# The down product of an expert moved one round later, next to the next expert's transpositions

## The reference, cut to what matters

```python
aff = jax.nn.softmax((xt @ w_router).astype(jnp.float32), axis=-1)
gate, idx = lax.top_k(aff.T, cap)          # cap = 64 tokens per expert and sequence
xe = xt[idx]
g = jnp.einsum('ecd,edf->ecf', xe, w_gate)
u = jnp.einsum('ecd,edf->ecf', xe, w_up)
ye = jnp.einsum('ecf,efd->ecd', jax.nn.silu(g) * u, w_down) * gate[..., None]
y = jnp.zeros_like(xt).at[idx.reshape(-1)].add(ye.reshape(-1, shp[-1]))
```

## Time and profile before

| | |
|---|---|
| Time, median of 3 runs (lowest to highest) | 2575.97 us (2575.56 to 2576.26) |
| The profiled execution: its own time, and its span | 2580.33 us, 2578.4 us |
| Busy, share of the span | PE 97%, PEld 54%, DVE 56%, ACT 21%, POOL 28% |
| The experts' stages, about | 604 to 1249 us and 1926 us to the end |

### The profile page before, as it was taken

How to read it: one execution, slowest core, us unless ns; L and a number is a source line. 1 busy time by engine, 2 the same in 40 slices (tenths; PEclk the granted TensorE clock), 3 DMA queues, 4 the chain that set the end, 5 groups by cost and what they waited for, 6 DMA issues and landing times. The chain is left out here.

```text
span 2578.4 us, 37067 instructions
## 1 busy us (share of the span) xinstructions
PE 2501.9 (97%) x13964; PEld 1383.5 (54%) x13964; DVE 1447.2 (56%) x2210; ACT 553.5 (21%) x1400; POOL 732.4 (28%) x797
## 2 busy tenths in 40 slices
PE   8999999999999999999799999999989999999998
PEld 4456556445555555565344554454446565555554
DVE  2465456347866767765125332533258767668674
ACT  2164146111111111111102330332111111111112
POOL 2276358114122121120004530553022121121212
PEclk9999999999999999999899999999989999999999
DMA  6100030337999999997600112014248999999996
GB/s 200 27 7 16 1 147 10 122 134 294 335 356 340 344 355 332 353 349 261 242 28 17 54 58 93 17 46 160 98 172 315 352 350 332 355 345 346 353 336 247
DMA packets 177342, 534.91 MB, mean 207 GB/s; under 512 B 32464, under 2 KB 47312, under 8 KB 177232
## 3 DMA queue, kind: packets, MB, share of 16 engines
q1 hardware_dynamic: 166432, 499.34, 51.7%
q0 software_dynamic: 10800, 34.09, 5.8%
HBM read 490.39 MB, written 44.56 MB: 207 GB/s over the span
## 5 line engine op out<-in xcount | busy, mean ns | idle before, releaser
L1858 PE MATMUL bank<-ring,arena 128*64 128x256 f32 x4096 | 479.8, 382 | 2.4 <-DVE arena L2134 1.9
L1869 PE MATMUL bank<-ring,arena 128*128 128x512 f32 x1024 | 451.3, 599 | 1.8 <-issue 0.9
L917 PE MATMUL bank<-ring,arena 128*128 128x512 f32 (+1 forms) x1024 | 429.8, 576 | 1.7 <-DMA ring<-in_w_in_cd 0.9
L1858 PEld LDWEIGHTS bank<-ring,arena 128*64 128x64 f32 x4096 | 291.8, 137 | 168.3 <-issue 30.2
L1570 POOL TENSOR_SCALAR arena<-arena 128x512 f32<-128x512 f32 (+2 forms) x256 | 328.0, 1298 | 185.6 <-DVE arena L1446 177.4
L1858 PE MATMUL bank<-arena 128*64 128x256 f32 x3072 | 364.6, 379 | 0.0
L934 PE MATMUL bank<-arena,ring 128*128 128x512 f32 x752 | 330.1, 597 | 4.0 <-DVE arena L1402 4.0
L1869 PEld LDWEIGHTS bank<-ring,arena 128*128 128x128 f32 x1024 | 193.2, 191 | 245.6 <-issue 244.5
L917 PEld LDWEIGHTS bank<-ring,arena 128*128 128x128 f32 x1024 | 193.2, 192 | 208.1 <-issue 201.3
L2191 POOL DMA_INDIRECT residual<-arena x30 | 83.4, 2779 | 741.7 <-DVE arena L2101 741.7
L1858 PEld LDWEIGHTS bank<-arena 128*64 128x64 f32 x3072 | 222.4, 137 | 109.7 <-issue 0.6
(11 more groups left out here) (215 smaller groups left out, 2210.2 us busy)
## 6 DMA issues: line engine op xcount, KB each, us to landing
ring<-in_w_gate SPq DMA_DIRECT2D x64, 2048.0 KB, 9.4
ring<-in_w_up SPq DMA_DIRECT2D x64, 2048.0 KB, 10.4
ring<-in_w_down SPq DMA_DIRECT2D x64, 2048.0 KB, 7.9
ring<-in_w_in_cd SPq DMA_DIRECT2D x6, 2048.0 KB, 17.3
ring<-in_x_in SPq DMA_DIRECT2D x16, 512.0 KB, 4.3
residual<-ring SPq DMA_DIRECT2D x16, 512.0 KB, 2.8
normed<-ring SPq DMA_DIRECT2D x16, 512.0 KB, 2.6
ring<-residual SPq DMA_DIRECT2D x16, 512.0 KB, 6.1
```

The lines of the kernel that those rows point to most:

```text
L917: mm = eng.matmul(bank[banks_of(piece)[k]][0:rows, 0:wide], lhs(c), rhs(c), start=(c == 0), stop=(c == chunks - 1))
L1858: mm = eng.matmul(bank[b][64 * h:64 * h + 64, first_column:first_column + 256], tokens[:, c, :], weights[:, c, 256 * h:256 * h + 256], sta ...
L1869: mm = eng.matmul(bank[6 + b][:, :], lhs[:, 4 * half + c, :], piece[k][:, c, b * BANK:(b + 1) * BANK], start=(half == 0 and c == 0), stop= ...
```

## The change

The down product lags by two rounds instead of one: a round is now g(e) in one piece, down(e-2), h(e-1), u(e). There is one more round: round 16 holds down(14) and h(15), round 17 down(15). The down weights of expert 15 are loaded into buffers 0 and 1, which the last gate product has left. On VectorE and ScalarE the copy to hT stands behind y instead of ahead of the weight differences and of silu. SyncE loads down(e-1) where it loaded down(e), and in the first layer fetches the next mixer's pieces in the order 2, 4, 5, 0, 1, 3 instead of 0, 1, 2, 3, 4, 5, with `first_x` between 5 and 0. In the last layer the residual's tiles go to buffers 4 and 5. The core of the diff:

```diff
-            lags = {"h0": 1, "h1": 1, "down lo": 1, "down hi": 1, "hT": 1, "y": 1, "index": 1, "gate": 1,
+            lags = {"h0": 1, "h1": 1, "hT": 1, "down lo": 2, "down hi": 2, "y": 2, "index": 2, "gate": 2,
...
-            pe_names = ["g1", "g6", "g2", "g7", "g5", "h0", "h1", "g3", "g4", "down lo", "down hi",
+            pe_names = ["g1", "g6", "g2", "g7", "g5", "g3", "g4", "down lo", "down hi", "h0", "h1",
                         "u1", "u6", "u2", "u7", "u5", "u3", "u4"]
...
-                xt, yt = (ring[:, k * PIECE:(k + 2) * PIECE].rearrange("p (n d) -> p n d", n=TILES) for k in (0, 2))
+                xt, yt = (ring[:, k * PIECE:(k + 2) * PIECE].rearrange("p (n d) -> p n d", n=TILES) for k in (4, 2))
...
-                for k in range(4):
-                    load(0, k, 1)
-                with eng.Fori(1, E - 1) as e:
+                def load_last_down(k):
+
+                    eng.wait_ge(pe_s.sem, pe_s.after(freed[k], E - 1))
+                    eng.dma_start(piece[k], at(w_down, (E - 1 + layer * E) * (D * F) + k * (D * F // 2), [[F, P], [P * F, 4], [1, F]])
+                                  ).then_inc(piece_in[k], 16)
+
+                for e in range(2):
+                    for k in range(4):
+                        load(e, k, 1)
+                with eng.Fori(2, E - 1) as e:
                     for k in (0, 1):
                         load(e, k, 1)
                     for k in (4, 5):
-                        load(e, k, 0)
+                        load(e, k, -1)
                     for k in (2, 3):
                         load(e, k, 1)
-                for k in (4, 5):
-                    load(E - 1, k, 0)
+                load_last_down(0)
+                load(E - 1, 4, -1)
+                load_last_down(1)
+                load(E - 1, 5, -1)
                 if first:
-                    for k in range(2):
-                        eng.wait_ge(pe_s.sem, pe_s.after(freed[k], E - 1))
-                        follow(eng, k)
                     eng.wait_ge(pe_s.sem, pe_s.after("u4", E - 1))
                     eng.dma_start(first_gain, at(norm_mix, (layer + 1) * D, [[0, P], [1, D]])).then_inc(first_in, 16)
                     follow(eng, 2)
+                    for k in (4, 5):
+                        eng.wait_ge(pe_s.sem, pe_s.after(freed[k], E - 2))
+                        follow(eng, k)
                     eng.wait_ge(scattered, 16 * (E - 1))
                     eng.dma_start(first_x, at(residual, 0, [[D, P], [1, D]])).then_inc(first_in, 16)
-                    for k in range(3, RING):
-                        eng.wait_ge(pe_s.sem, pe_s.after(freed[k], E - 1))
+                    for k in range(2):
+                        eng.wait_ge(pe_s.sem, pe_s.after(("down lo", "down hi")[k], E - 1))
                         follow(eng, k)
+                    follow(eng, 3)
...
                     if "g1" not in left_out:
                         eng.wait_ge(dve_s.sem, dve_s.after("xT", e))
                         products("g", "s4", "tg2")
+                        last_products("g", "tg4")
+                    if "down lo" not in left_out:
+                        eng.wait_ge(act_s.sem, act_s.after("hT", e - 2))
+                        eng.wait_ge(dve_s.sem, dve_s.after("hT", e - 2))
+                        eng.wait_ge(act_s.sem, act_s.after("y", e - 3))
+                        eng.wait_ge(dve_s.sem, dve_s.after("y", e - 3))
+                        product(hT, 0 if is_end(e) else 4, 0, "down lo", e - 2)
+                        product(hT, 1 if is_end(e) else 5, 1, "down hi", e - 2)
```

More of the change, by code:

```diff
@@ L1783, in is_end, with behind, ahead @@
             def is_end(e):
-                return isinstance(e, int) and e == E
+                return isinstance(e, int) and e == E + 1
             def rounds(steps, eng, body):
-                late = [m for m in steps.names if lags.get(m) == 1]
                 early = [m for m in steps.names if lags.get(m) == -1]
-                tail = [m for m in steps.names if lags.get(m) != 1]
-                steps.part(late)
-                body(0, 0, late)
+                def behind(rounds):
+                    return [m for m in steps.names if lags.get(m, 0) >= rounds]
+                def ahead(rounds):
+                    return [m for m in steps.names if lags.get(m, 0) < rounds]
+                steps.part(behind(1))
+                body(0, 0, behind(1))
+                steps.part(behind(2))
+                body(1, 1, behind(2))
                 steps.part()
-                body(1, 1, ())
-                with eng.Fori(1, E // 2 - 1) as pair:
+                body(2, 0, ())
+                body(3, 1, ())
+                with eng.Fori(2, E // 2 - 1) as pair:
                     for j in range(2):
@@ L1800, in rounds @@
                 body(E - 1, 1, early)
-                steps.part(tail)
-                body(E, 0, tail)
+                steps.part(ahead(1))
+                body(E, 0, ahead(1))
+                steps.part(ahead(2))
+                body(E + 1, 1, ahead(2))
             def sp(eng):
@@ L1913, in body @@
                             pe_s.done(f"h{i}", mm)
[L1914 to L1920, removed]
                     if first and is_end(e):
                         eng.wait_ge(choice_made, 1)
-                        eng.wait_ge(act_s.sem, act_s.after("y", e - 1))
-                        eng.wait_ge(dve_s.sem, dve_s.after("y", e - 1))
+                        eng.wait_ge(act_s.sem, act_s.after("y", e - 2))
+                        eng.wait_ge(dve_s.sem, dve_s.after("y", e - 2))
                         for k in range(2):
-                            eng.matmul(bank[2 + k][:, :], choice, y[1 - j][0:64, k * 512:(k + 1) * 512], start=True, stop=True).then_inc(placed, 1)
+                            eng.matmul(bank[2 + k][:, :], choice, y[j][0:64, k * 512:(k + 1) * 512], start=True, stop=True).then_inc(placed, 1)
                     if "u1" not in left_out:
@@ L1977, in body @@
                     if "y" not in left_out:
[L1979 to L1981 removed]
+                        eng.wait_ge(pe_s.sem, pe_s.after("down hi", e - 2))
+                        eng.wait_ge(pool_s.sem, pool_s.after("gate", e - 2))
+                        act_s.done("y", eng.activation(y[j][:, 0:512], bank[6][:, :], ACT.Copy, scale=gate[j]))
+                    if "hT" not in left_out:
+                        eng.wait_ge(pe_s.sem, pe_s.after("h0", e - 1))
+                        act_s.done("hT", eng.activation(hT[:, :, 0:64], bank[0][:, :].rearrange("p (c t) -> p c t", t=64), ACT.Copy))
                     if "u p1" not in left_out:
@@ L2040, in body @@
                 def body(e, j, left_out):
-                    if "hT" not in left_out:
-                        eng.wait_ge(pe_s.sem, pe_s.after("h1", e - 1))
-                        dve_s.done("hT", eng.tensor_copy(hT[:, :, 64:128], bank[1][:, :].rearrange("p (c t) -> p c t", t=64)))
                     if last and is_end(e):
@@ L2097, in body @@
                         combine("g", 3, e + 1)
+                    if "tg2" not in left_out:
+                        for n in (2, 4):
+                            combine("g", n, e + 1)
                     if "y" not in left_out:
-                        eng.wait_ge(pe_s.sem, pe_s.after("down hi", e - 1))
-                        eng.wait_ge(pool_s.sem, pool_s.after("gate", e - 1))
-                        dve_s.done("y", eng.tensor_scalar(y[1 - j][:, 512:1024], bank[7][:, :], gate[1 - j], None, ALU.mult))
+                        eng.wait_ge(pe_s.sem, pe_s.after("down hi", e - 2))
+                        eng.wait_ge(pool_s.sem, pool_s.after("gate", e - 2))
+                        dve_s.done("y", eng.tensor_scalar(y[j][:, 512:1024], bank[7][:, :], gate[j], None, ALU.mult))
+                    if "hT" not in left_out:
+                        eng.wait_ge(pe_s.sem, pe_s.after("h1", e - 1))
+                        dve_s.done("hT", eng.tensor_copy(hT[:, :, 64:128], bank[1][:, :].rearrange("p (c t) -> p c t", t=64)))
                     if first and is_end(e):
```

58 lines of the change are left out of this document (26 added, 32 removed).

## The result

| | before | changed |
|---|---|---|
| Median of 8 runs each (lowest to highest) | 2577.45 us (2575.56 to 2581.12) | 2583.35 us (2581.58 to 2586.72) |
| Ratio, with its 95% interval | | 1.0024 [1.0015, 1.0034] |
| Profiled execution: its time, its span | 2580.33, 2578.4 us | 2584.28, 2582.5 us |

The change costs 5.9 us, 0.24%, with an interval of 3.9 to 8.8 us. I had forecast +1.9 us. The time lies inside my range, just outside what I called no change.

The account below looks back on a forecast made before the run. TensorE was taken to bound the rounds, other chains the ends. Rounds -9.0, round 1 +9.0, clock +2.0, layer 1's end -7.0, program's end +6.9 gave +1.9 us: median 2577.9 us, range 2571 to 2586.

Parts of the forecast that it names:

- what I called no change: Whole kernel: a median within 0.2%, 5.2 us, of the one before, that is 2570.8 to 2581.1 us; chance 0.59.
- rounds: Rounds 1 to 15 of each layer: one change of TensorE's form less saves 0.30 us a round, -9.0 us in all.
- The bound that let the price hang on the down product: Rounds: if the form change's price hangs on down, only h's 0.15 us a round is saved, -2.3 us per layer.
- round 1: Round 1 of each layer: without a down product TensorE waits 1.75 and 2.7 us in up, +9.0 us over both.
- clock: Behind round 1's two waits: TensorE's clock may fall, 1.0 us per layer, +2.0 in all, bounds 0 and 4.
- end of layer 1: Layer 1's end and next mixer: TensorE's 2.19 us wait goes, scatter and rows come earlier, -7.0 us, bounds -3.7 and -7.5.
- rival 3: Mixer behind layer 1: gains only the earlier start's 3.6 us if rows don't pass the weights, 2581.2 us; chance 0.10.
- the end of the program: Last layer's end: y(14) comes 12.1 us later, its scatter takes 5.0 instead of 10.16 us: +6.9 us, bounds +5.3 and +12.1.
- Rival 2: Program's end: the scatter stays at 10.16 us because reading and adding rows takes its time, 2583.1 us; chance 0.10.

Follow-up runs that it names:

- e3: The changed kernel with transpositions h back in the middle of the gate product, the down product left late: 2598.24 us, 1.0083.
- e4: The changed kernel with up block 6 waiting for tu2, two up copies ahead of silu, and hT last on ScalarE: 2575.67 us, 0.9996.
- e5: The changed kernel with the next mixer's weight piece 3 asked for right behind piece 2 in layer 1's end: 2579.38 us, 1.0009.
- e6: The changed kernel without expert 14's scatter in the last layer, tile loads waiting for u(15), tile buffers swapped: 2569.63 us, 0.9969.
- e2: The kernel before with the change made in the second layer's experts only: 2585.97 us, 1.0039.
- e7: The kernel before with its first layer changed plus the edits of e4 and e5, last layer as before: 2567.46 us, 0.9963.
- c1: The changed kernel measured once more, with nothing altered: 2583.27 us, 1.0024 against the kernel before.
- e1: The kernel before with the change made in the first layer's experts only: 2576.11 us, 0.9993.
- e8: The kernel before without expert 14's scatter in the last layer, tile loads waiting for the end of u(15): 2576.8 us, 0.9999.

## Why the prediction was right and wrong

**Right, rounds.** "0.29, say 0.30 us a round" was 0.305, and e3 undoes exactly that. The bound that let the price hang on the down product is refuted.

**Right, round 1.** Waits of 1.75 and 2.7 were 1.86 and 2.76, at the blocks and for the engines named. It was a chain of single VectorE and ScalarE operations of known length behind the start of `hidden`, and could be added up. e4 takes most of it away.

**Right in the mean, clock.** A fall after two short waits was forecast at 1.0 per layer; it was 1.7 in layer 2 and nothing in layer 1. The sum of 2.0 was close by luck as much as by reading.

**Wrong, end of layer 1: -7.0 was -3.2.** The step that failed is "so both the scatter (3.6 earlier) and the load behind it (lands near 1257 instead of 1264) gain". The first half held (3.5). The load landed about 1258.4, which looks like the forecast, but 2.98 us of that was chance at the stage's start; without it the load would have landed about 1261.4 and rival 3 was true, the case to which I gave 0.10. I had added up three weight pieces at 386 GB/s from 1237 us and put their end at 1254, 3 us before the rows were needed. In the rows the transfers ran at 355 to 360 GB/s and were still at a share of 0.92 until 1258.4. The scatter of expert 15 ran beside the pieces (1242.91 to 1252.20), and towards its landing, from 1248 to 1252 us, the transfers moved only 264 to 286 GB/s where they had moved 394 from 1240 to 1244; that it was the scatter which slowed them is likely and was not tested. e5 confirms that the rows stood behind the weights: with one piece fewer ahead of them, the wait of 2.40 us becomes 0.49.

**Right in kind, too small: the end of the program, +6.9 was +8.0.** That the rows of expert 14 carry the end is shown by e6, and that they cost some 10 us with all else of layer 2 by e2. The prediction said that down(15) had no part in the chain; it was 0.3 us away from it. The term mis-sized is the scatter, 5.0 taken between bounds of 3.4 and 10.16, 6.1 measured; what came back was 4.1 instead of 5.2. Rival 2, the scatter unchanged at 10.16, was false: with no other transfer beside it it is faster. This window of the changed kernel holds it:

```profile
2537.00:2551.20 14.20, 13.30 (x37) 6.17 (x36) 1.45 (x2) 1.18 (x2) 1.57 (x1) 1.00 0.24 37
```

37 GB/s over 14.2 us are 0.52 MB, the scatter's own rows; every byte of the window is on its queue. In the kernel before, the transfers moved 300 GB/s in all while it was under way (2537.00 to 2547.40).

**The sum.** Of the 4.7 us between the ledger's 6.6 and my 1.9, 3.8 are the end of layer 1 and 1.1 the scatter. The rounds, the clock and the two waits nearly cancel. I don't put the side of the error down to chance: where I could add up operations of one engine, the numbers held to 0.1 us; where I divided bytes by a rate that one busy window showed, I took the best rate and no other queue.

## What to carry to other kernels

Before moving work later in the last round, list every way that reaches the end and its distance to the longest. Here two lay 0.3 us apart, so making one of them earlier brought nothing and making the other later cost all of it. A lag added for a gain in the steady rounds has a price once per stage, in the round where the moved work is missing: add up there what it used to cover on the other engines. Then see whether their order can pay it back, as e4 did; and make the change only in the stage whose end can bear it, as e7 did.

## What the runs showed of the hardware

- TensorE pays 0.30 us for one excursion from the 64-column form to the full one and back: 20.87 + 1.02 + 3.60 + 13.93 against 24.32 + 13.93 + 0.87. That is 9 us of this kernel.
- An indirect DMA that adds 128 rows of 4 KB to HBM took 6.1 us with no other transfer beside it (6.0 in e2), where a plain indirect write of as many rows to y_out took 3.4. The adding is what differs by the code; no run changes it alone.
- Two waits of 1.68 and 2.54 us with one block product between them were followed by the 1.2 GHz clock in layer 2 and not in layer 1, with the same waits to the hundredth. Each layer has the two waits in six traces (the first of 1.68 to 2.18 us, the second of 2.53 or 2.54). The clock fell behind them in layer 2 in all six (the changed kernel, c1, e2, e3, e5, e6), and in layer 1 in two of six (e1 and e5; not in the changed kernel, c1, e3, e6). Whether it falls can't be read from the waits alone; what a fall cost can, 1.71 us here.
- Two microseconds at a stage's start came and went with the clock between executions of unchanged code: the first gate block took 3.68 us in the kernel before and 1.95 in e8, whose first layer is the same. Such luck added up to 4.2 us here (2.98 and 1.2), so a smaller difference between two profiled spans of this kernel is not a result.
